# Neighbourhood attention: where the softmax is divided by its row sum

## The reference, cut to what matters

```python
s_nb = s_nb.reshape(bsz, GRID_W, H, n_nb)
s_ctx = jnp.einsum('bqhd,bchd->bqhc', q_r, k_ctx).astype(jnp.float32) * scale
p = jax.nn.softmax(jnp.concatenate([s_nb, s_ctx], axis=-1), axis=-1).astype(v.dtype)
p_nb = p[..., :n_nb].reshape(bsz, GRID_W, H, wr, WIN_COLS)
p_ctx = p[..., n_nb:]
return (jnp.einsum('bqhpj,bpqjhd->bqhd', p_nb, v_win)
        + jnp.einsum('bqhc,bchd->bqhd', p_ctx, v_ctx))
```

## Time and profile before

| what | value |
|---|---|
| times of three runs | 1729.97, 1724.52, 1725.44 us; median 1725.44 |
| span of the profiled execution | 1727.8 us |
| PE matmul busy | 1685.5 us, 98% of the span |
| DVE, ACT, POOL busy | 51%, 45%, 37% |
| mean granted clock of TensorE | 0.992 |

### The profile page before, as it was taken

The page is one execution under the profiler, slowest core; times in us unless marked ns, Lnnn a source line. Parts: engine busy times, 40 slices in busy tenths (PEclk is TensorE's granted clock), DMA queues, the critical chain, the costliest instruction groups (busy, mean ns, idle before and its releaser), DMA issues. The chain is left out here.

```text
span 1727.8 us, 27062 instructions
## 1 busy us (share of the span) xinstructions
PE 1685.5 (98%) x10190; PEld 1431.6 (83%) x10190; DVE 884.8 (51%) x1554; ACT 772.0 (45%) x1366; POOL 631.1 (37%) x439
## 2 busy tenths in 40 slices
PE   7999999999999999999999999999999999999998
PEld 6987777778888889988997788798787788989896
DVE  4223333344445328947645565687544575555552
ACT  5324554532223334556545655444445324626251
POOL 1007665633330076742103422866200227414242
PEclk9999999999999999999999999999999999999999
DMA  7231221223334223243731111223511223222221
GB/s 318 100 96 37 73 79 49 73 104 121 109 111 146 98 73 118 103 162 134 290 130 65 52 47 50 85 104 133 216 50 50 98 73 114 107 98 97 97 98 49
DMA packets 29800, 181.65 MB, mean 105 GB/s; under 512 B 3352, under 2 KB 5784, under 8 KB 10112
## 3 DMA queue, kind: packets, MB, share of 16 engines
q1 hardware_dynamic: 22136, 150.12, 24.0%
q10 hardware_dynamic: 7560, 30.09, 4.9%
HBM read 169.57 MB, written 10.50 MB: 104 GB/s over the span
## 5 line engine op out<-in xcount | busy, mean ns | idle before, releaser
L409 PE MATMUL acc<-rarena,wh 128*128 128x512 f32 (+1 forms) x1720 | 659.1, 383 | 10.5 <-DVE farena L1863 2.8
L410 PE MATMUL acc<-rarena,wh 128*128 128x512 f32 (+1 forms) x1720 | 643.7, 374 | 0.0
L411 PE MATMUL acc<-rarena,wl 128*128 128x512 f32 (+1 forms) x1720 | 643.5, 374 | 0.0
L409 PEld LDWEIGHTS acc<-rarena,wh 128*128 128x128 f32 x1720 | 324.7, 189 | 91.9 <-issue 26.7
L411 PEld LDWEIGHTS acc<-rarena,wl 128*128 128x128 f32 x1720 | 324.6, 189 | 62.8
L410 PEld LDWEIGHTS acc<-rarena,wh 128*128 128x128 f32 x1720 | 324.9, 189 | 56.8 <-issue 0.5
L312 DVE TENSOR_TENSOR wl<-raw,wh 128x2048 fp32r<-128x2048 f32 x85 | 207.0, 2435 | 259.5 <-ACT wh L306 259.4
L306 ACT ACTIVATE wh<-raw 128x2048 fp32r<-128x2048 f32 x103 | 196.5, 1908 | 76.2 <-PE acc L411 69.4
L312 POOL TENSOR_TENSOR wl<-raw,wh 128x2048 fp32r<-128x2048 f32 x18 | 82.6, 4586 | 153.2 <-ACT wh L306 153.2
L2495 POOL TENSOR_TENSOR wl<-raw,wh 128x512 fp32r<-128x512 f32 x78 | 104.9, 1373 | 91.5 <-ACT wh L1281 91.5
L487 PE MATMUL acc<-wh,rarena 128*128 128x256 f32 x384 | 109.1, 284 | 4.0 <-DVE rarena L1738 2.5
(11 more groups left out here) (320 smaller groups left out, 2904.2 us busy)
## 6 DMA issues: line engine op xcount, KB each, us to landing
raw<-in_w SPq DMA_DIRECT2D x129, 1024.0 KB, 4.8
early<-in_wmod SPq DMA_DIRECT2D x8, 1024.0 KB, 19.7
farena<-in_gate ACTq DMA_DIRECT2D x4, 1024.0 KB, 4.7
mkv_scratch<-rarena ACTq DMA_DIRECT2D x2, 2048.0 KB, 12.5
rarena<-mkv_scratch ACTq DMA_DIRECT2D x1, 4096.0 KB, 13.3
farena<-in_rpb ACTq DMA_DIRECT2D x16, 240.0 KB, 3.8
farena<-in_x_grid SPq DMA_DIRECT2D x2, 1024.0 KB, 8.0
o_scratch<-early ACTq DMA_DIRECT2D x8, 256.0 KB, 2.0
```

The costliest lines, as they stand in the source:

```text
L409: mm(o, w[0], m[0], start=start, stop=False)
L410: mm(o, w[0], m[1], start=False, stop=False)
L411: return mm(o, w[1], m[0], start=False, stop=stop)
```

## The change

DVE takes each head's reciprocal as soon as its exponentials and their row sum are there, and multiplies the 128 x 512 exponentials by it in place. PE waits for that (`rinv_done`) and not for `exp_done` before the transposes. The spread on PE, its copy on ACT and the product on DVE go; the block output is copied from PSUM by DVE. Counts of `ot_done` and `ot_hi` in later stages start 32 lower.

```diff
@@ PE, attend_nb
                     if made(j - 1):
-                        pe.wait_ge(s_("rinv_done"), g)
-                        W(pe, "ot_free", n - 1)
-                        spread_rinv(j - 1, O[j % 2]).then_inc(s_("ot_done"), 1)
+                        W(pe, "ot_free", n - 2)
                         for a in range(2):
                             pe.wait_ge(s_("phi_done"), g - 1 + a)
                         values_nb(it, pc, j - 1, O[(j - 1) % 2])
...
-                            pe.wait_ge(s_("exp_done"), g + 1 + a)
+                            pe.wait_ge(s_("rinv_done"), g + 1 + a)
@@ ACT, attend_nb
-                    if made(j - 1):
-                        act.wait_ge(s_("ot_done"), n)
-                        W(act, "ot_free", n - 2)
-                        f(rspread[j % 2], O[j % 2][:, 128:256], ACT.Copy).then_inc(s_("ot_hi"), 1)
@@ DVE, attend_nb
-                    if made(j - 1):
-                        cc = (2 * j - 2) % 8
-                        v.wait_ge(s_("exp_done"), g)
-                        nc.vector.reciprocal(rinv[:, cc:cc + 2], rowsum[:, cc:cc + 2]).then_inc(s_("rinv_done"), 2)
...
+                        for a in range(2):
+                            cc = 2 * j + a
+                            v.wait_ge(s_("exp_done"), g + 1 + a)
+                            link(nc.vector.reciprocal(rinv[:, cc:cc + 1], rowsum[:, cc:cc + 1]))
+                            ts(ptile[a], ptile[a], rinv[:, cc:cc + 1], None, MUL).then_inc(s_("rinv_done"), 1)
                     if j in (0, 2) and not last_pair:
                         rope(it, pc + 1, j // 2)
...
-                        v.wait_ge(s_("ot_hi"), n)
                         v.wait_ge(s_("pv_done"), g)
-                        tt(stage[pr % 2][:, 128 * qb:128 * qb + 128], O[(j - 1) % 2][:, 0:128], rspread[j % 2], MUL)\
+                        nc.vector.tensor_copy(stage[pr % 2][:, 128 * qb:128 * qb + 128], O[(j - 1) % 2][:, 0:128])\
                             .then_inc(s_("ot_free"), 1)
```

More of the change, by code:

```diff
@@ L175, in build @@
         wmask = F(21.5, 3, 256)
-        rspread, unbiased = [F(24.5, 128), F(25, 128)], F(27.5, 256)
+        unbiased = F(27.5, 256)
         c_t, u_t, y_t, sg_t = F(0, 2, SEQ), F(4, 2, SEQ), F(8, 2, SEQ), F(12, 2, SEQ)
@@ L335, in build @@
         PAIRS, SLOTS, G2 = 8, 32, 64
+        NB_BLOCKS = 32
         def after(m):
@@ L621, in values_nb @@
                             last.then_inc(s_("pv_done"), 1)
[L623 to L628, removed]
             def scores_causal(m):
@@ L1488, in attend_causal @@
                 if u >= 0:
-                    act.wait_ge(s_("ot_done"), 32 + u + 1)
+                    act.wait_ge(s_("ot_done"), u + 1)
                     pr, qb = divmod(u, 4)
@@ L1518, in attend_causal @@
                         act.wait_ge(s_("rinv_done"), after(p) - 1 + a)
-                        W(act, "ot_done", 32 + p - 17)
+                        W(act, "ot_done", p - 17)
                         f(osb2[p % 2][:, 64 * a:64 * a + 64], O[a][:, 0:64], ACT.Copy, scale=rinv[:, cc:cc + 1])\
@@ L1638, in attend_mm @@
                         j, pr = (i - 3) % 4, pc - 1 if i < 3 else pc
-                        act.wait_ge(s_("ot_done"), MM.ot0 + 4 * pc + i - 3 + 1)
+                        act.wait_ge(s_("ot_done"), MM.ot0 - NB_BLOCKS + 4 * pc + i - 3 + 1)
                         f(om[0][:, 2 * pr:2 * pr + 2, 128 * j:128 * j + 128],
@@ L1645, in attend_mm @@
                         act.wait_ge(s_("rinv_done"), g - 1)
-                        W(act, "ot_done", MM.ot0 + 4 * pc + i - 3)
+                        W(act, "ot_done", MM.ot0 - NB_BLOCKS + 4 * pc + i - 3)
                         f(osbm[a], O[a][:, 0:256], ACT.Copy, scale=rinv[:, j:j + 1]).then_inc(s_(f"o_free{a}"), 1)
@@ L1908, in _ @@
             with v.Fori(0, 2) as it:
+                own.loop(it, 16)
                 for pc in (3, 4):
                     attend_nb(it, pc, False, False)
+            own.done(2)
             attend_nb(0, 7, False, True)
@@ L2173, in attend_causal @@
                 if u >= 0:
-                    v.wait_ge(s_("ot_hi"), 32 + u + 1)
+                    v.wait_ge(s_("ot_hi"), u + 1)
                     pr, cols = u // 4, slice(128 * (u % 4), 128 * (u % 4) + 128)
@@ L2318, in attend_mm @@
                         j, pr = (i - 3) % 4, pc - 1 if i < 3 else pc
-                        v.wait_ge(s_("ot_hi"), 48 + 4 * pc + i - 3 + 1)
+                        v.wait_ge(s_("ot_hi"), MM.ot0 - NB_BLOCKS + 4 * pc + i - 3 + 1)
                         cols = slice(128 * j, 128 * j + 128)
```

## The result

The changed kernel takes 1758.36 us in the median of 4 runs (1755.68 to 1763.96), the kernel before 1726.56 of 4 (1724.52 to 1729.97). The ratio is 1.0189, with a 95% interval of 1.0166 to 1.0212. The prediction was 1757, from 1738 to 1776. The profiled execution has a span of 1754.4 us and a mean granted clock of 0.986 (before 1727.8 and 0.992).

A forecast was written before the change was run, and what follows sets the result against it. PE's own work was taken to bound the attention, with ACT and DVE delivering within slack. Waits from POOL's hold, net of the spread's saving, gave +20 us and the clock +12: from 1725.44 to 1757 us, range 1738 to 1776.

The forecast's parts named there:

- The hold: Block 0 of each pair: DVE's scaling waits for POOL's whole 4.58 us weight-job instruction, from 222.65 to 227.09.
- Block 0: Each pair's first block: PE reaches the second head's transposes 2.75 us late.
- the first pair: First pair of heads, block 0: second scaling waits for POOL's whole split, 4.1 us in place of 2.75, +1.3.
- Blocks 1 to 3: Rest of each pair: spread saves 0.27 us a block, POOL's short pieces fit, 0.1 lost in block 3.
- The spread: PE's products spreading the reciprocals: removal saves 0.27 us per block, 8.6 us in all.
- The scaling beside nothing: DVE's multiplication of 128 x 512 by a column, undisturbed: 0.54 us, hidden in the first six pairs.
- The seventh pair: Its last block, without a projection to cover it: delayed rotation and two POOL pieces of 1.28 us cost +2.7 us.
- The clock: After PE's new waits: seven stretches of 3.4 us at half clock, +12 us, bounds 0 and 31.
- the rival with the clock up: Attention: POOL holds the scalings but PE's clock does not fall; 1745 us, chance 0.20.
- Who waits: PE before the transposes waits for DVE's scaling: eight or nine waits of about 3 us, 20 to 30 in all.
- The sum: Whole kernel: +20 us from the attention and +12 from the clock, +32 us, median 1757 us.
- The rival on the other side: Attention: POOL does not hold the scaling, so the spread's 8.6 us less 1 are gained; 1718 us, chance 0.12.

The follow-up runs named there:

- e4: Changed kernel with the exponentials left in PSUM and scaled by DVE from there into the SBUF tile; 1722.94 us, ratio 0.9974.
- e7: Changed kernel with 20 unread products on PE ahead of the transposes of block 0 in each pair; 1747.16 us, ratio 1.0126.
- e1: Changed kernel with POOL's low part of the weight job in block 0 waiting until both heads' exponentials are scaled; 1724.81 us, ratio 0.9986.
- e2: e1 with the two spread products per block put back on PE, their results unread; 1729.67 us, ratio 1.0012.
- e6: e4 with DVE's rotation in blocks 0 and 2 moved ahead of the two scalings; 1723.78 us, ratio 0.9982.
- e3: Changed kernel with POOL's low part of the weight job in block 0 issued as four instructions instead of one; 1725.17 us, ratio 0.9985.
- e5: Kernel before with 64 multiplications of 128 x 512 added on DVE, on a scratch tile nobody reads; 1730.32 us, ratio 1.0022.

## Why the prediction was right

- **The hold.** Forecast from 222.65 against POOL's 222.51, 0.14 us too late; in that pair it came 0.14 us late. The bounds were nothing and one whole instruction, and the upper one holds. In pairs 1 and 8 DVE won the race and the second head was held, and the loss was there all the same, as the prediction said. By the rule of the Trainium skill named in the prediction the sum was the same, and now a row shows the case it speaks of: a tensor_scalar of SBUF beside GpSimd, 4.69 us in place of 0.49. The same page ("SBUF — State Buffer", "Who interferes with whom") says that an instruction with at most one SBUF input and outside the two-port modes does not contend; e4's 750 to 752 ns beside POOL agree.
- **Block 0.** Forecast +2.75, counted to the second head's transposes. Measured +2.33 to the first head's, and by e7, whose clock stays up, another 0.22 for the second head, which falls into the step of block 1 (6.89 us against 6.67 in e1): +2.55. In the first pair the second head's transposes come 3.5 us late, forecast 4.1.
- **Blocks 1 to 3.** Forecast -0.27 and -0.17 for blocks 2 and 3; measured -0.23 and -0.25. POOL's short pieces do hold scalings there (1.55 us at most), inside the slack. Block 1 was forecast near 6.6 us and took 8.29: the loss by the clock stood in the sum, but was put into no step, and this is the step in which it lies.
- **The spread.** Forecast 0.27 us a block, 8.6 in all. The steps show 0.22 to 0.25, and nothing where PE waits; e2 gives 4.9 us by the medians and 5.4 by the profiles, so as the gain of a kernel without waits this term was over by more than a third. The 0.27 was read from the start of one group to the start of the next, and the values take 0.05 us longer without the spread ahead of them.
- **The scaling beside nothing.** Forecast 0.54, from an instruction with two columns; 0.49 with one column. Hidden where PE has other work, as e1 shows.
- **The seventh pair.** Forecast +2.7 for its last block; 6.50 us after, against 3.78. The number is right, and in part by luck: of the two holds that were put in, only one shows (1.49 us behind L2418; the second head's scaling takes 0.49), and in its place the exponentials come 1.0 us later after the transposes of block 2 than before, because ACT waits for the sum of the delayed rotation on POOL. e4, without any hold, still has 6.09 us there, and e6, with the rotation ahead, 4.85. This part is in e1 and e4 too, and with the smaller spread it is why they gain some 2 to 4 us and not 7.6.
- **The clock.** Forecast seven stretches of 3.4 us, 12 us. The records show seven of that length, one after the long wait of each of the first seven pairs, and two more, of 6.8 us behind the seventh pair's last block and of 3.4 behind the eighth pair's first; e7 puts the price at 11. How many of the waits would count was a guess from two rows, the least founded term, and that it fell so close is luck. One of the two rows was itself chance: the wait of 1.75 us at 1170.92, on which the rival with the clock up leaned, has no stretch behind it in the profiles of the kernel before, of the changed kernel and of e7; in the other eight the same wait (1.76 to 1.90 us) is followed by one of 3.4 us.
- **Who waits.** Forecast eight or nine waits, 20 to 30 us: ten of the weight loads, 27.4 us.
- **The sum.** Forecast 20 and 12; the profiles of the attention give 30.1, the medians 31.8. The profiled execution was forecast at about 1762 us and took 1756.11, since the one before was slow by its opening (clock 0.94 against 0.98) and the one after was not. In the attention the sum was 2 us over: block 0 by 0.2 us a pair, the first pair by 0.6 and the clock by about 1, with the spread, of which only blocks 1 to 3 count here, by less than 1 on the other side. That the median came within 1.4 us of 1757 is luck at that size: the runs of either kernel lie 5 to 8 us apart.

The rival on the other side, 1718 us, asked that POOL should not hold the scaling. e1, e3 and e4, where it does not or hardly does, give 1723 to 1725: that rival was itself too low by 5 to 7 us, through the spread (some 3) and the seventh pair.

## What to carry to other kernels

Before an elementwise step is moved to an idle DVE, look at what POOL runs at that moment and how long its longest single instruction is: if the two exclude each other, as the in-place scaling and POOL's operations did here, the step takes as long as that instruction, whatever DVE's busy share says. Three cheap ways out were worth 33 to 35 us each here: let the long one start after the short one, cut the long one in pieces, or read from PSUM. And a wait of PE costs more than its length, since what follows may run at half clock.

## What the runs showed of the hardware

- The in-place scaling of 128 x 512 takes 485 ns alone and 0.75 us out of PSUM; the PSUM form did not vary by more than 2 ns beside POOL.
- In e5 DVE's record starts at 223.85, in the tail of POOL's bias operation, and POOL's long one at 223.89; POOL still went first, and so in two more pairs with a lead of 0.04 to 0.05 us. With a lead of 0.11 to 0.14 us DVE went first.
- The hold works both ways: where DVE went first, POOL's L312 took 4.70 to 4.82 us and not 4.55 to 4.62, and in e3 its pieces took 1.47 us beside the scalings and 1.28 without.
- Twenty products whose results nobody reads made the kernel 11 us faster, by keeping the granted clock at 1.00 over a wait. It is not a remedy, since e1 does without the wait.
